# Moving adaLN chunk loads and dot products in the two attention projections of layer 0

## The reference

```python
mod_lat = jax.nn.silu(c) @ w_ada[l] + b_ada[l]          # 6 x 1024 modulation values per layer
shift1, scale1, gate1, shift2, scale2, gate2 = jnp.split(mod, 6, axis=-1)
h = modulated_norm(x, norm_mix, shift1, scale1)
u = h @ w_in                                            # u_hy, u_na, u_da, u_gate
y_hy, y_na, y_da = hyena(u_hy), neighbourhood_attention(u_na), diff_attention(axial_rope(u_da))
merged = g[0] * (y_hy @ w_lift[0]) + g[1] * (y_na @ w_lift[1]) + g[2] * (y_da @ w_lift[2])
x = x + gate1 * (merged @ w_out)
h2 = modulated_norm(x, norm_ffn, shift2, scale2)
x = x + gate2 * ((silu(f_gate) * f_up) @ w_ffn_out)
```

## Time and profile before

| | us |
|---|---|
| device time, median of 3 runs | 2985.23 (2985.14 to 2987.11) |
| profiled execution, device time | 2975.47 |
| its span, first to last instruction | 2973.6 |
| TensorE matmuls busy | 2823.4 (95%) |
| VectorE busy | 1430.7 (48%) |
| ScalarE busy | 754.1 (25%) |
| GpSimd busy | 1596.7 (54%) |
| mean granted TensorE clock | 0.974 of full speed |

### The profile page before, as it was taken

The page is one execution under the profiler, slowest core; times in us unless marked ns, Lnnn a source line. Parts: engine busy times, 40 slices in busy tenths (PEclk is TensorE's granted clock), DMA queues, the critical chain, the costliest instruction groups (busy, mean ns, idle before and its releaser), DMA issues.

```text
span 2973.6 us, 42669 instructions
## 1 busy us (share of the span) xinstructions
PE 2823.4 (95%) x17704; PEld 2550.6 (86%) x17704; DVE 1430.7 (48%) x2267; ACT 754.1 (25%) x1411; POOL 1596.7 (54%) x596
## 2 busy tenths in 40 slices
PE   7889899989999999999999989999999999999998
PEld 2349687978888999999998869797988998999998
DVE  6555685664545235477646571542455425411113
ACT  3442112215564112000112110414555212000110
POOL 0426132364434776788875507075333675777775
PEclk9979999999999999999999999899999999999999
DMA  5422242231111323345422213021111233322222
GB/s 218 138 96 95 92 161 88 96 92 43 52 46 61 114 70 123 113 156 163 144 91 88 92 59 102 5 93 54 46 52 52 84 96 107 98 73 78 72 78 79
DMA packets 80093, 272.12 MB, mean 92 GB/s; under 512 B 8955, under 2 KB 14715, under 8 KB 78108
## 3 DMA queue, kind: packets, MB, share of 16 engines
q1 hardware_dynamic: 48124, 168.77, 17.8%
q10 hardware_dynamic: 31776, 100.62, 9.8%
HBM read 245.76 MB, written 23.59 MB: 91 GB/s over the span
## 4 chain that ended last, share of the span: by engine, by line
PE 80%; DVE 9%; ACT 4%; issue 2%; DVEq 1%; DMA 1%; POOLq 1%; POOL 1%; ACTq 0%; SPq 0%
PE PS L499 46%; PE PS L843 9%; PE PS L562 4%; PE PS L636 3%; PE PS L892 2%; PE PS L509 2%; PE PS L790 2%; DVE adap L1483 2%; PE PS L864 1%; PE PS L774 1%; POOLq L482 1%; PE PS L602 1%; POOL wlo L483 1%; PE PS L759 1%; PE PS L869 1%
## 5 line engine op out<-in xcount | busy, mean ns | idle before, releaser
L481 POOL TENSOR_SCALAR whi<-wraw 128x1024 fp32r<-128x1024 f32 x284 | 819.2, 2884 | 1146.6 <-PE PS L499 635.5
L483 POOL TENSOR_TENSOR wlo<-wraw,whi 128x1024 fp32r<-128x1024 f32 x292 | 734.4, 2515 | 83.3 <-ACT whi L1246 38.9
L499 PE MATMUL PS<-hhi,whi 128*128 128x320 f32 x2432 | 556.7, 310 | 15.7 <-POOL wlo L483 15.7
L499 PE MATMUL PS<-hhi,wlo 128*128 128x320 f32 x2432 | 554.7, 309 | 0.0
L499 PE MATMUL PS<-hlo,whi 128*128 128x320 f32 x2432 | 554.7, 309 | 0.0
L499 PEld LDWEIGHTS PS<-hhi,whi 128*128 128x128 f32 x2432 | 407.2, 188 | 18.4 <-POOL wlo L483 11.5
L499 PEld LDWEIGHTS PS<-hlo,whi 128*128 128x128 f32 x2432 | 407.8, 188 | 0.0
L499 PEld LDWEIGHTS PS<-hhi,wlo 128*128 128x128 f32 x2432 | 407.4, 188 | 0.0
L1483 DVE CUSTOM_DVE_ANT_0 adap<-ada,cond 128x1024 f32<-128x1024 f32 x176 | 333.2, 1893 | 36.1 <-DMA ada<-in_w_ada 14.7
L1401 ACT ACTIVATE silu<-PS 128x640 f32<-128x640 f32 x44 | 31.2, 708 | 659.1 <-PE PS L499 655.8
L1915 DVE TENSOR_TENSOR gact<-silu,PS 128x640 f32<-128x640 f32 x44 | 36.1, 821 | 333.3 <-ACT silu L1401 333.3
(11 more groups left out here) (294 smaller groups left out, 5022.8 us busy)
## 6 DMA issues: line engine op xcount, KB each, us to landing
wraw<-in_w_strips SPq DMA_DIRECT2D x292, 512.0 KB, 3.5
ada<-in_w_ada ACTq DMA_DIRECT2D x80, 512.0 KB, 4.6
spectra<-hst ACTq DMA_DIRECT2D x48, 256.0 KB, 2.1
hld<-spectra ACTq DMA_DIRECT2D x8, 768.0 KB, 5.0
hld<-spectra ACTq DMA_DIRECT2D x12, 512.0 KB, 3.6
part<-hacc ACTq DMA_DIRECT2D x8, 640.0 KB, 3.5
macc<-part ACTq DMA_DIRECT2D x8, 640.0 KB, 4.1
pada<-in_w_ada ACTq DMA_DIRECT2D x8, 512.0 KB, 3.7
```

What stands on the lines that cost most here:

```text
L481: nc.gpsimd.tensor_scalar(hi, raw, 1.0, None, ALU.mult)
L483: nc.gpsimd.tensor_tensor(lo, raw, hi, ALU.subtract).then_inc(w_split, 1)
L499: ins = pe.matmul(out[:, h, :], w[:, kt, :], mv[:, h * HALF:(h + 1) * HALF], start=start and m == 0, stop=stop and m == 2)
```

## The change

In layer 0 the chunk loads and dots stand at other places of the streams; no work is added or dropped apart from one wait.

- Neighbourhood projection, ScalarE: the pair of chunk loads behind eviction n is the pair that stood behind eviction n-1, so chunks 3 and 4 are loaded behind eviction 3 and chunks 11 and 12 behind eviction 7. Chunks 13, 14 and 15 are loaded one at a time behind the high parts made beside the value strips.
- Differential projection, VectorE: a rotation is no longer preceded by a chunk. Chunks 0, 1 and 2 are taken after rotations 1, 3 and 5, chunks 3 to 7 after the last rotation.
- Differential projection, ScalarE: chunks 2 and 3 are loaded behind evictions 4 and 6, chunks 4 to 7 behind the last eviction.
- Before its first exponential of the differential attention ScalarE waits until all eight dots of set 3 are done, because the attention's buffers share memory with the chunks'.

```diff
@@ -1250,15 +1250,15 @@
                     act.wait_ge(s_nq, nth(lay, s_nq, n + 1))
                     dst, sc = (naq, -0.125) if n < 4 else (nak, 1.0)
                     A(halves(dst[:, n % 4, :]), pair((n + 3) % 4), ACT.Copy, scale=sc).then_inc(s_nqe, 1)
-                    for k in range(max(2 * n - 1, 3), 2 * n + 1):
+                    for k in range(max(2 * n - 3, 3), 2 * n - 1):
                         if lay == 0:
                             ada_load(1, k, (lay, N_ADA1 + k))
-                if lay == 0:
-                    ada_load(1, 15, (lay, N_ADA1 + 15))
                 act.wait_ge(s_nqe, nth(lay, s_nqe, 8))
                 act.dma_start(a["new_na_k"][lay], nak[:, :, 0:C]).then_inc(s_ko, 16)
                 for n in range(8, N_NA):
                     strip_hi(lay * STRIPS + S_NA + n + 1)
+                    if lay == 0 and n < 11:
+                        ada_load(1, n + 5, (lay, N_ADA1 + n + 5))
                 act.wait_ge(s_nv, nth(lay, s_nv, 1))
                 for i in range(NT):
                     A(nav[:, i, :], PS[:, i, :], ACT.Copy).then_inc(s_nve, 1)
@@ -1295,8 +1295,11 @@
                         act.wait_ge(s_drope, nth(lay, s_drope, n - 1))
                     A(halves(draw[n % 2][:, :]), pair((n + 3) % 4), ACT.Copy,
                       scale=-DA_SCALE if n < 4 else 1.0).then_inc(s_dqe, 1)
-                    if lay == 0 and 1 <= n < KD - 1:
-                        ada_load(3, n + 1, (lay, 2 * KD + n + 1))
+                    if lay == 0 and n in (4, 6):
+                        ada_load(3, n // 2, (lay, 2 * KD + n // 2))
+                for k in range(4, KD):
+                    if lay == 0:
+                        ada_load(3, k, (lay, 2 * KD + k))
                 act.wait_ge(s_drope, nth(lay, s_drope, 8))
                 act.dma_start(a["new_da_k"][lay], dak[:, :, 0:C]).then_inc(s_ko, 16)
                 act.wait_ge(s_dv, nth(lay, s_dv, 1))
@@ -1345,6 +1348,7 @@
                     act.dma_start(part[mp], hacc[:, :, :]).then_inc(s_spill, 16)
 
                 kept = 0
+                act.wait_ge(ada_used[3], KD)
                 for n in range(41):
                     if n < 40:
                         da_exp(n, 0)
@@ -1750,10 +1754,6 @@
 
                 for n in range(8):
                     dst, r = (daq, daq, daq, daq, dak, dak, dak, dak)[n], draw[n % 2]
-                    if lay == 0:
-                        if n == 0:
-                            dve.wait_ge(s_cond[2], 16)
-                        ada_dot(3, n, 2 * KD + n)
                     dve.wait_ge(s_dqe, nth(lay, s_dqe, n + 1))
                     dve.drain()
                     V.stream_shuffle(dsw[:, :], r[:, C:T], [i ^ 1 for i in range(32)])
@@ -1763,6 +1763,13 @@
                     V.tensor_tensor(dsw[:, :], dsw[:, :], ropes[:, :], ALU.mult)
                     dve.drain()
                     V.tensor_tensor(dst[:, n % 4, C:T], dst[:, n % 4, C:T], dsw[:, :], ALU.add).then_inc(s_drope, 1)
+                    if lay == 0 and n in (1, 3, 5):
+                        if n == 1:
+                            dve.wait_ge(s_cond[2], 16)
+                        ada_dot(3, n // 2, 2 * KD + n // 2)
+                if lay == 0:
+                    for k in range(3, KD):
+                        ada_dot(3, k, 2 * KD + k)
 
                 def da_max(n):
                     p0, q = 0 if n // HEADS else 512, 2 * (n % 2)
```

## The result

| | before | after |
|---|---|---|
| device time, median (us) | 2985.23 | 2968.38 |
| ratio to before, with 95% interval | | 0.9942 (0.9926 to 0.9957) |
| profiled execution, device time (us) | 2975.47 | 2967.03 |
| its span (us) | 2973.6 | 2965.2 |

A forecast was written before the change was run, and what follows sets the result against it. TensorE's own work was taken as 80% of the span, so only its waits and lower clock could pay: 7.3 us neighbourhood plus 9.0 differential, 16.3, off the 2985.2 median gives 2968.9 us; range 2966 to 2977.

The forecast's parts named there:

- 8.1 us less 0.8: Layer 0 neighbourhood projection: 6.3 us of waits and 1.8 of clock removed, 0.8 us residual wait over four steps; net 7.3.
- The free 2.3 us: Neighbourhood projection: ScalarE's hold past a strip's end that costs nothing, 7.04 less high half, low half and hand-overs.
- Pace is no limit: Neighbourhood projection: claimed VectorE's chunk pace doesn't bind; 13 chunks took 47 us before, 3.6 each, two a strip.
- This cover: Neighbourhood projection's end: VectorE's dots finish 2 to 7 us before the first maximum; any excess is lost one for one.
- 9.0 us forecast: Layer 0 differential projection: 6.8 us of waiting for the last eviction and 2.2 of clock removed.
- the two-ended estimate of rotations 4 and 5: Differential projection: rotation 4 ends at 602 to 607, needed at 612.2; rotation 5 at 610 to 612, needed at 619.2.
- the tail: Differential projection: chunks 3 to 7 behind the last rotation, modulation sum by 646, 6 us of cover; at worst 12 late.
- The two clock terms, 1.8 and 2.2 us: Lower-clock losses behind TensorE's waits of 3.6 us (neighbourhood projection, 1.8) and 7.6 us (differential projection, 2.2).
- a wait of 3.6 us or more: TensorE waits in both projections: one this long costs some 2 us extra through lower clock, one of 1.3 us nothing.
- The rival of ScalarE's hold: Neighbourhood projection: ScalarE still held, two steps wait some 2 us more each, giving back 4 us: 2973; chance 0.15.
- The rivals: ScalarE held 2973 (0.15), tail 8 us late 2979 (0.07), both halves 3000 (0.03), gain absorbed by later waits 2985 (0.04).
- both halves of a strip hold VectorE: Differential projection: GpSimd's high and low halves both shut VectorE out, tail 29 us late: 3000 us; chance 0.03.

The follow-up runs named there:

- The lengthened tail: Changed kernel with the two dots of chunk 7 taken four times more before layer 0's differential attention; that attention took 321.8 us against 309.6 to 311.3.

## Why the prediction was right, point by point

**Neighbourhood projection: right in size, the residual for another reason.** 8.1 us less 0.8 were forecast and 8.0 were measured in the profile. From TensorE's start to the end of the value strips it is 86.0 us (397.83 to 483.82), against 8 x 7.04 + 0.8 + 28.27 = 85.4 undisturbed, so 0.6 us are left, and the stage had lost 8.6 us before, 0.5 more than was priced. ScalarE is still held in each step, by 2.2 to 2.7 us past the strip's end, where 0.3 to 3.3 were worked out:

```profile
440.12 2.61 ACTq L1040 DMA_DIRECT2D ada<-in_w_ada  x2
...
442.83 1.06 ACT L1246 ACTIVATE whi<-wraw 128x1024 fp32r<-128x1024 f32 x1 [2.02 <-DVE mraw L1487]
...
454.80 2.71 ACTq L1040 DMA_DIRECT2D ada<-in_w_ada  x2
```

```profile
443.97 3.35 POOL L483 TENSOR_TENSOR wlo<-wraw,whi 128x1024 fp32r<-128x1024 f32 x1 [4.05 <-ACT whi L1246]
```

Strip 5's sum is evicted at 440.11; the high half comes at 442.83, 2.7 us later, the low half ends at 447.32, and TensorE goes on at 447.47, a few tenths late. The free 2.3 us were used up. But what held ScalarE was not the landing from which the prediction had worked it out. After its first chunk VectorE waits for no landing in this stage; from 430.42 on its dots stand back to back, and in these steps every fourth one is held up by a low half:

```profile
437.79 3.22 DVE L1487 CUSTOM_DVE_ANT_0 adap<-ada,cond 128x1024 f32<-128x1024 f32 x1
...
445.20 3.19 DVE L1487 CUSTOM_DVE_ANT_0 adap<-ada,cond 128x1024 f32<-128x1024 f32 x1
...
452.60 3.19 DVE L1487 CUSTOM_DVE_ANT_0 adap<-ada,cond 128x1024 f32<-128x1024 f32 x1
```

Two chunks take 7.40 us, a strip 7.04. The loads, the high halves and at last the strips follow VectorE's pace: the last three evictions of the loop are 7.27 and 7.41 us apart (440.11, 447.38, 454.79). "Pace is no limit" was wrong, by its own figures too: 3.6 us a chunk and two a strip are 7.2. That the hold worked out from landings came out in the right range is luck; with four such steps it cost some 0.6 us. VectorE's modulation sum behind its last chunk, and the first maximum of the attention:

```profile
480.34 0.18 DVE L1502 SCALAR_TENSOR_TENSOR amod<-mod,pars 128x16 f32<-128x16 f32 x1
...
485.57 0.49 DVE L1697 TENSOR_REDUCE mx<-PS 128x1 f32<-128x128 f32 x2 [5.05 <-PE PS L762]
```

The idle time went from 15.41 us to 5.05 us; 2 to 7 us were forecast. This cover held.

**Differential projection: right.** 9.0 us forecast, 8.5 measured in the profiles. The half us is left in the strips, 56.57 us against 56.33 undisturbed and 28.50 against 28.27; what delays them there shows in no wait and stays open. The evictions came on time up to the last, as the two-ended estimate of rotations 4 and 5 had said. Of the tail, VectorE's rows from the last rotation on, the row of ScalarE's last four loads and one of GpSimd:

```profile
622.39 0.69 DVE L1765 TENSOR_TENSOR dak<-dak,dsw 128x512 f32<-128x512 f32 x1
...
626.54 1.23 DVE L1487 CUSTOM_DVE_ANT_0 adap<-ada,cond 128x1024 f32<-128x1024 f32 x1
...
627.90 1.84 DVE L1487 CUSTOM_DVE_ANT_0 adap<-ada,cond 128x1024 f32<-128x1024 f32 x1
...
644.63 2.18 DVE L1494 TENSOR_TENSOR mod<-mraw,pars 128x16 f32<-128x16 f32 x1
...
651.66 0.42 DVE L1779 TENSOR_REDUCE mx<-PS 128x2 f32<-128x256 f32 x1 [4.84 <-PE PS L862]
```

```profile
618.42 18.36 ACTq L1040 DMA_DIRECT2D ada<-in_w_ada  x4
```

```profile
626.82 3.58 POOL L481 TENSOR_SCALAR whi<-wraw 128x1024 fp32r<-128x1024 f32 x1 [1.48 <-PE PS L562]
```

The last rotation ended at 623.1, or 4.7 us after the eighth strip's end at 618.4 (4.8 forecast). The modulation sum ended at 646.8 and the idle time is 4.84 us, where 6 were forecast; the sum alone took 2.18 us beside a low half. ScalarE stood in its four loads for 18.36 us, until 636.8, 10.9 us before the value eviction (12 forecast). The lengthened tail showed that the cover was needed: past it, each us is lost.

**The price of a wait: right in size, wrong in its lower end.** The two clock terms, 1.8 and 2.2 us, came back but for 0.2 us, and all waits of the study put the loss at 1.2 to 2.7 us. That "a wait of 3.6 us or more" costs it was all that the rows before could show; the runs showed it from 2.3 us on. The rival of ScalarE's hold may therefore have been priced too low: its two waits of about 2 us lie between 1.6 us, which cost no clock, and 2.3 us, which did.

**The rivals.** None came true. For "both halves of a strip hold VectorE" the profile after repeats the argument: the dot instruction of 627.90, begun inside the high half of 626.82, took 1.84 us, as before. Held until that half's end at 630.40, it would have taken 3.7; the low half does hold a dot so (3.2 us). The other way round VectorE does hold the high half. This one took 3.58 instead of 2.77 us, because the dot of 626.54 had 0.95 us to go when it began; three more that began beside a running dot took 3.63 to 3.81. The Trainium skill's rule ("SBUF — State Buffer", section "Who interferes with whom") that the second one blocks fully agrees with the low half, and nearly with a high half that comes second; it does not agree with a dot that comes second to a high half, and this rival needed that case.

**The total.** 16.3 us forecast, 17 by the medians, 16.5 by the two stages. That the median lies within 1 us of the forecast is partly luck: the two stages missed by +0.7 and -0.5 us, and the two later comparisons of the changed kernel with the kernel before gave 17 and 13 us by the ratio. The part that a reader could not have forecast from one profile is the level: the profiled execution of the kernel before was 10 us below its median, through stages that the change does not touch. To carry the gain to the median, not the level, was what kept the number right.

## What to carry to other kernels

A load whose buffer must first come free holds all that stands behind it on the queue that issues it: put it behind the work that others wait for, and one step later than seems necessary. Compare the pace of the engine that frees the buffers with the step, too: 7.40 against 7.04 us left 0.6 us here. Work that is not urgent goes behind the step that releases the next engine, not ahead of it, and a part of it past the last such step, up to the idle time that the trace shows there. What a wait of TensorE costs is its length plus what the clock takes behind it; a twin stage without the disturbance shows both in one comparison.

## What the runs showed of the hardware

- The granted clock fell behind a wait of TensorE of 2.3 us, not behind one of 1.6 us; the loss was 1.2 to 2.7 us for waits of 2.3 to 11.6 us, and not larger behind the longest.
- The neighbourhood attention took 75.3, 78.3 and 79.5 us in three profiles of the changed kernel. This goes with how long the lower clock level lasts at its start: in the same 7 us, begun 16 us after the first value eviction, 1.00, 0.52 and 0.50 were granted.
- A dot instruction of VectorE (1.23 us alone) that began 0.2 to 1.1 us into GpSimd's high half took 1.84 to 1.93 us, one that began 2 us or more into it 1.23, and one that began up to 1.2 us into a low half 3.1 to 3.4; a high half that began beside a running dot waited for most of the dot's rest (3.58 to 3.81 us instead of 2.77).
- The 394 to 404 us ahead of the neighbourhood projection vary by 10 us among profiles of kernels with the same instructions there; what decides it was not looked into and stays open.
